# Modulation product of a two-layer diffusion step on four column tiles of TensorE

## What is computed

```python
def _adaln(cond, w, b):
    m = jax.nn.silu(cond) @ w + b
    return jnp.split(m[:, None, :], 3, axis=-1)

h = _rmsnorm(x, lp['norm_g']) * (1.0 + scale) + shift
z = h @ lp['w_in']
...
x = x + gate * (mixed @ lp['w_out'])
```

## Time and profile before

| what | value |
|---|---|
| median of the runs | 848.39 us |
| span of the profiled execution | 845.0 us (3.4 below the median) |
| TensorE busy | 712.7 us, 84% |
| VectorE busy | 605.8 us, 72% |
| ScalarE busy | 316.0 us, 37% |
| GpSimd busy | 172.6 us, 20% |
| moved by DMA | 117.64 MB, mean 139 GB/s |
| chain that ended last, by engine | TensorE 52%, VectorE 36%, ScalarE 3%, DMA 3% |

### The profile page before, as it was taken

How to read it: one execution, slowest core, us unless ns; L and a number is a source line. 1 busy time by engine, 2 the same in 40 slices (tenths; PEclk the granted TensorE clock), 3 DMA queues, 4 the chain that set the end, 5 groups by cost and what they waited for, 6 DMA issues and landing times.

```text
span 845.0 us, 9392 instructions
## 1 busy us (share of the span) xinstructions
PE 712.7 (84%) x3294; PEld 469.8 (56%) x3294; DVE 605.8 (72%) x1103; ACT 316.0 (37%) x563; POOL 172.6 (20%) x121
## 2 busy tenths in 40 slices
PE   4957899990779994988999999999907698999996
PEld 1145665550721533776778558655507456787785
DVE  3378689997355589768866554899973568888664
ACT  1244451111323322454655355401213433545552
POOL 1067449202000009033000100492020000000000
PEclk9979999995789997999999999999967698999999
DMA  6864335350067471554565475454220034555661
GB/s 208 282 146 118 125 128 173 110 145 28 3 155 232 141 239 61 150 150 146 154 184 168 147 236 165 137 166 118 73 99 1 26 99 124 176 174 155 195 177 55
DMA packets 79339, 117.64 MB, mean 139 GB/s; under 512 B 27437, under 2 KB 31869, under 8 KB 79293
## 3 DMA queue, kind: packets, MB, share of 16 engines
q1 hardware_dynamic: 78460, 116.52, 45.6%
q10 hardware_dynamic: 832, 0.53, 0.3%
HBM read 112.51 MB, written 1.38 MB: 135 GB/s over the span
## 4 chain that ended last, share of the span: by engine, by line
PE 52%; DVE 36%; ACT 3%; DMA 3%; issue 2%; SPq 2%; POOL 1%; DVEq 0%; ACTq 0%; POOLq 0%
PE proj L1032 11%; PE proj L1034 10%; PE proj L1033 10%; DVE H L1358 8%; PE proj L730 8%; DVE cvacc L1423 7%; DVE qkt L1358 7%; PE side L765 4%; PE proj L756 3%; DVE qM_split L1358 3%; PE side L963 2%; DVE wide_split L1358 2%; DMA raw<-in_w_ada 2%; DVE H L1575 2%; DVE gates_split L1358 2%
## 5 line engine op out<-in xcount | busy, mean ns | idle before, releaser
L756 PE MATMUL proj<-raw,hT 128*128 128x512 f32 (+1 forms) x320 | 125.1, 551 | 0.0
L1423 DVE SCALAR_TENSOR_TENSOR cvacc<-cvpad,taps,cvacc 128x256 f32<-128x256 f32 x240 | 123.1, 541 | 0.0
L1358 DVE TENSOR_TENSOR wide_split<-raw,wide_split 128x512 fp32r<-128x512 f32 x118 | 90.6, 773 | 41.4 <-ACT wide_split L1086 40.3
L1086 ACT ACTIVATE wide_split<-raw 128x512 fp32r<-128x512 f32 x118 | 74.4, 632 | 95.9 <-PE proj L1034 95.9
L756 PEld LDWEIGHTS proj<-raw,hT 128*128 128x128 f32 x320 | 60.3, 190 | 60.4 <-issue 58.4
L730 PE MATMUL proj<-raw,cond 128*2 128x512 f32 x192 | 88.8, 617 | 5.9 <-DMA raw<-in_w_ada 5.9
L1358 DVE TENSOR_TENSOR H<-H,qkt 128x128 f32<-128x128 f32 x128 | 75.5, 590 | 1.2
L1032 PE MATMUL proj<-wide_split,H_split 128*128 128x512 f32 x154 | 65.0, 422 | 13.2 <-DVE wide_split L1358 12.7
L1783 POOL TENSOR_SCALAR st<-st 128x1 f32<-128x1 f32 (+1 forms) x12 | 3.9, 324 | 336.9 <-DVE st L1692 148.7
L961 PE MATMUL side<-qM,Uz 128*64 128x64 f32 x128 | 20.5, 248 | 54.3 <-DVE HY L1676 54.3
L1033 PE MATMUL proj<-wide_split,H_split 128*128 128x512 f32 x154 | 62.8, 408 | 0.0
(11 more groups left out here) (235 smaller groups left out, 1491.1 us busy)
## 6 DMA issues: line engine op xcount, KB each, us to landing
raw<-in_w_in SPq DMA_DIRECT2D x104, 512.0 KB, 3.8
raw<-in_w_ada SPq DMA_DIRECT2D x48, 512.0 KB, 4.5
raw<-in_w_out SPq DMA_DIRECT2D x16, 512.0 KB, 4.2
raw<-in_w_ssm_glu SPq DMA_DIRECT2D x8, 512.0 KB, 5.2
raw<-in_w_ssm_out SPq DMA_DIRECT2D x8, 512.0 KB, 3.8
raw<-in_w_attn_out SPq DMA_DIRECT2D x8, 512.0 KB, 4.1
raw<-in_w_conv_out SPq DMA_DIRECT2D x8, 512.0 KB, 3.9
raw<-in_w_in SPq DMA_DIRECT2D x8, 256.0 KB, 2.8
```

Of the source, the lines that this page charges most:

```text
L756: m = T.matmul(proj.bank((l, u, s))[:, 0:n], lhs[:, s, kt, :], w[:, i, :], start=(kt == 0), stop=last)
L1086: S.activation(chunk_parts(m)[0], chunk_raw(m), ACT.Copy).then_inc(chunk_hi, 1)
L1358: return V.tensor_tensor(out, a, b, op)
L1423: m = V.scalar_tensor_tensor(acc, src, taps[:, t, j:j + 1], acc, ALU.mult, ALU.add)
```

## The change

The stationary operand `cond` is made 32 columns wide, the two conditioning vectors repeated 16 times. Each slab is multiplied in four matmuls of 256 columns; matmul j writes partitions 32j to 32j + 31 of one bank, which is column tile j of TensorE's array. ScalarE copies the bank in one piece of 128 x 256 into a buffer of its own, two full transposes bring it to columns, and VectorE's addition picks the two wanted rows out of each 32. The ScalarE waits on the shared buffer go. The order of stages is the same. The launch reserves a smaller scratch for DMA descriptors.

```diff
 ADA_PARTS = 3
-ADA_BANKS = D // W
+ADA_COLS = D // 4
+ADA_ROWS = P // 4
 MERGE_OF = {"A": 0, "B": 1, "C": 2}
...
         condrow = rows[:, 0, P:2 * P]
-        cond = sb("cond", [P, NS, DT])
+        cond = sb("cond", [P, DT, ADA_ROWS])
         h0 = sb("h0", [P, ROW])
...
 
-        adarow = th[:, 2:4, :].rearrange("p a b -> p (a b)")
+        adarow = sb("adarow", [P, ADA_COLS])
         qk = sb("qk", [P, NS, QK])
...
             if stg[0] == "ada":
-                proj_uses += [(stg + (b,), 1) for b in range(ADA_BANKS)]
+                proj_uses.append((stg, 1))
             proj_uses += [((l, u, s), 1) for u, _, _ in units_of(stg) for s in range(NS)]
...
             elif key[:-1] + (key[-1] + 1,) not in {q[0] for q in slabs}:
-                last = ADA_BANKS - 1 if key[0] == "ada" else NS - 1
-                slab_read.append((proj.full, proj.at[key[:-1] + (last,)][0] + 1))
+                bank_of = key[:-1] if key[0] == "ada" else key[:-1] + (NS - 1,)
+                slab_read.append((proj.full, proj.at[bank_of][0] + 1))
             else:
...
                 if kt == 0:
-                    for b in range(ADA_BANKS):
-                        proj.claim(pe, stg + (b,))
+                    proj.claim(pe, stg)
                 slab_landed(pe, stg + (kt,))
                 w = slab_view(stg + (kt,))
-                for b in range(ADA_BANKS):
-                    m = T.matmul(proj.bank(stg + (b,))[0:NS, :], cond[:, :, kt], w[:, 0, W * b:W * b + W],
-                                 start=(kt == 0), stop=(kt == DT - 1))
-                    if kt == DT - 1:
-                        m.then_inc(proj.full, 1)
-                if kt < DT - 1:
-                    m.then_inc(slab_used, 1)
+                for j in range(4):
+                    m = T.matmul(proj.bank(stg)[ADA_ROWS * j:ADA_ROWS * j + ADA_ROWS, 0:ADA_COLS], cond[:, kt, :],
+                                 w[:, 0, ADA_COLS * j:ADA_COLS * j + ADA_COLS], start=(kt == 0), stop=(kt == DT - 1))
+                m.then_inc(proj.full if kt == DT - 1 else slab_used, 1)
 
...
                 elif k == "adaT":
-                    for b in range(ADA_BANKS):
-                        proj.drained(pe, ("ada",) + stg[1:] + (b,))
+                    proj.drained(pe, ("ada",) + stg[1:])
                     side.claim(pe, stg)
-                    for t in range(DT):
-                        m = transpose(side.bank(stg)[:, NS * t:NS * t + NS], adarow[0:NS, P * t:P * t + P])
+                    for t in range(ADA_COLS // P):
+                        m = transpose(side.bank(stg)[:, P * t:P * t + P], adarow[:, P * t:P * t + P])
                     m.then_inc(side.full, 1)
...
                     side.filled(act, ("cond",))
-                    S.activation(cond[:, :, :].rearrange("p s t -> p (s t)"), side.bank(("cond",))[:, 64:80],
-                                 ACT.Silu).then_inc(cond_done, 1)
+                    S.activation(cond[:, :, :].rearrange("p t (i s) -> p s t i", s=NS),
+                                 side.bank(("cond",))[:, 64:80].rearrange("p (s t) -> p s t", s=NS).unsqueeze(3)
+                                 .to_broadcast([P, NS, DT, ADA_ROWS // NS]), ACT.Silu).then_inc(cond_done, 1)
                 elif k in ("ada", "adaEnd") and stg != OVER_EDGE:
...
                         side.filled(act, ("adaT",) + ada_parts[ada_parts.index(stg) - 1][1:])
-
-                    for u in {("ada", 0, 2): ("glua",), OVER_EDGE: ("wo0", "wo1")}.get(stg, ()):
-                        for s in range(NS):
-                            proj.drained(act, (0, u, s))
-                    for b in range(ADA_BANKS):
-                        key = stg + (b,)
-                        proj.filled(act, key)
-                        S.activation(adarow[0:NS, W * b:W * b + W], proj.bank(key)[0:NS, :],
-                                     ACT.Copy).then_inc(proj.freed(key), 1)
+                    proj.filled(act, stg)
+                    S.activation(adarow[:, :], proj.bank(stg)[:, 0:ADA_COLS], ACT.Copy).then_inc(proj.freed(stg), 1)
                 elif k == "cT":
...
                         high_parts(ahead(l, "cg"))
-                        if l:
-                            side.filled(act, ("adaT", l, 2))
-                    if stg[1] == "glub" and l + 1 < DEPTH:
-                        side.filled(act, ("adaT", l + 1, 1))
                     for s in range(NS):
...
                 elif k == "comb":
-                    if stg == ("comb", BRANCHES[0], 0) and l == 0:
-                        side.filled(act, ("adaT", 0, 2))
                     unit = stg[1] + str(stg[2])
...
                     part = slice(DT * c, DT * c + DT)
-                    tt_(ada[:, ll, part, :], side.bank(stg)[:, 0:NS * DT].rearrange("p (t s) -> p t s", s=NS),
-                        modc[:, ll, part].unsqueeze(2).to_broadcast([P, DT, NS]), ALU.add).then_inc(side.freed(stg), 1)
+                    tiles = ADA_COLS // P
+                    tt_(ada[:, ll, part, :].rearrange("p (j t) s -> p t j s", t=tiles),
+                        side.bank(stg)[:, 0:ADA_COLS].rearrange("p (t j q) -> p t j q", t=tiles, j=4)[:, :, :, 0:NS],
+                        modc[:, ll, part].rearrange("p (j t) -> p t j", t=tiles).unsqueeze(3)
+                        .to_broadcast([P, tiles, 4, NS]), ALU.add).then_inc(side.freed(stg), 1)
                     if c == 1:
...
 
-    nc = bacc.Bacc("TRN2", target_bir_lowering=False, num_devices=1)
+    nc = bacc.Bacc("TRN2", target_bir_lowering=False, num_devices=1, dynamic_dma_scratch_size=1024)
     arrays = {}
...
     def given(prefix, named):

```

## The result

The changed kernel takes **833.53 us** (median of 4 runs, 832.25 to 834.15); the kernel before took 847.51 beside it (4 runs, 846.03 to 848.56). The ratio is 0.9845, 95% interval 0.982 to 0.9869: faster by about 14 us. The forecast was 831.0, range 822 to 847. The profiled execution's span is 831.2 us against 845.0, so 13.8 us have to be found in the trace.

What follows compares the result with a forecast made beforehand. TensorE and DMA were taken as nearly balanced, the gain bounded by the DMA. Start 7, middle 7, after the GLU 0 and edge 3.3 sum to 17.3 us, carried to the 848.39 median: 831 us, range 822 to 847.

Steps and rivals of the forecast that it cites:

- The array: Modulation product: column tiles overlap in part, so a slab costs TensorE 0.86 us, between bounds of 0.43 and 2.59.
- Serial tiles: Modulation product: the four tiles run one after another, 1.71 us per slab as before; 846.3 us, chance 0.10.
- Exposed weight loads: Every product but four slabs: weight loads no longer hide, 2.59 us per slab instead of 1.71; 885.0 us, chance 0.07.
- Start: First 16 slabs and the input transposes behind them: the stretch shortens by 5.5 to 8.5 us, taken as 7.
- the limit that the prediction put at 5.5: Kernel start: SyncE issues its last w_ada slab, then b loads and first w_in slab, only some 5.5 us earlier.
- Middle: Middle of layer 0, 4 + 8 slabs: GELU transposes start at 269.0 instead of 275.6; 7 us with shorter transposes.
- after the GLU: Eight slabs behind the GLU: VectorE reaches its addition straight behind its taps without waiting; 0 us, 3 either way.
- side cases of the prediction: Middle of layer 0: GELU up to 2.6 us sooner; or slabs take 1.5 us and TensorE is late by a microsecond.
- 0.4 from fewer transposes: Middle of layer 0, at the GELU transposes: fewer transposes save 0.4 us, part of the 7 us there.
- Edge: Between the layers, 4 + 4 slabs: first half hides, first w_in slab released earlier, shorter transposes; 3.3 us.
- Release at 487.2, 3.1 earlier: Between the layers: the fifth slab's use releases the first w_in slab at 487.2 instead of 490.26; 3.1 us.
- The clock rival: TensorE, idle between slabs, drops to 1.2 GHz and a slab takes 1.71 us even overlapped; 843.5 us, chance 0.03.

Runs made afterwards that it cites:

- half slabs: Changed kernel loading only 512 of the 1024 columns of each w_ada slab, each half multiplied twice; 821.67 us, ratio 0.9711 to the kernel before.
- two-tile kernel: Changed kernel with each slab's four matmuls, from the second k-tile on, going in pairs to the first two column tiles; 832.39 us.
- one-tile: Changed kernel with all four matmuls of a slab, from the second k-tile on, going to the first column tile; 839.99 us.
- edge-filled kernel: Changed kernel with 10, 6 and 20 matmuls that nobody reads added in TensorE's idle time between the layers; 830.34 us.

## Why the prediction was right

**The array.** The forecast rested on tiles that overlap, at 0.86 us a slab between bounds of 0.43 and 2.59. It is 0.43 at the upper clock and at most 0.87 where 0.54 was granted (with half slabs, four in 3.47 us from 25.46), both under the transfer, so that the choice between them was without effect, as the two-tile kernel shows. That 0.87 is near the forecast's 0.86 is luck: the prediction had it from tiles that overlap in part. *Serial tiles* are refuted by the 288 us row (0.43, not 1.71). *Exposed weight loads* too: eight loads are hidden in each slab of that row. Here the Trainium skill ("TensorE: Matmul & The Clock Gate", Part 3, What overlaps and what doesn't) let loads pass a running matmul only where the row group differs; these share one row group and pass. The prediction's estimate from that part, 0.54 us a slab, was near in size but above what the row shows.

**Start, 7 us forecast, 5.7 measured** (4.1 to 5.7 over the profiles with the same start). First use of the fifth slab at 19.73 (landing 19.1 forecast), then 1.51 us a slab rather than 1.4, 11 x 0.11 = 1.2 us: the pace of four buffers; six have 1.28. The input transposes, forecast near 37 us, begin at 40.72, behind those of `pre`, 5.3 us sooner than before. What sets the term is the limit that the prediction put at 5.5, SyncE's advance and GpSimd behind it. SyncE, then GpSimd's first block:

```profile
40.77 16.14 SPq L663 DMA_DIRECT2D raw<-in_w_in  x6
...
66.16 2.71 POOL L1766 TENSOR_TENSOR pre<-tA,tB 128x1024 f32<-128x1024 f32 x1
```

The first w_in slab goes 4.4 us sooner than before and GpSimd's block ends 3.7 us sooner. The chain of waits now runs through the b loads and this block; before, it ran through the product and VectorE's splits.

**Middle, 7 us, and after the GLU, 0; together 6.2.** TensorE's and ScalarE's timelines:

```profile
262.21 1.08 PE L730 MATMUL proj<-raw,cond 128*32 128x256 f32 x8 [0.47 <-DMA raw<-in_w_ada]
263.23 1.97 PE L762 MATMUL side<-ident,mixed 128*128 128x128 f32 x8
264.99 0.63 PE L762 MATMUL side<-ident,adarow 128*128 128x128 f32 x2
265.42 1.14 PE L905 MATMUL side<-kz,qM 128*128 128x512 f32 x2
```

```profile
259.32 0.63 ACT L1296 ACTIVATE mixed<-mixed 128x512 f32<-128x512 f32 x1 [0.70 <-DVE mixed L1342]
```

With the start's 5.7 us added, so on the clock of the kernel before, the GELU transposes begin at 268.95; 269.0 was forecast. The number held, its reason did not: GELU is through at 259.95, 3 us ahead, and TensorE is last, because the twelve slabs took 1.52 us each. Both were side cases of the prediction (GELU sooner, slabs at 1.5), and that they met at the same number is luck. The "0.4 from fewer transposes" became 0.6 more: 2.2 us from 263.23 to 265.42, at a granted clock of 0.50, against 1.6. Behind the GLU, VectorE reaches its addition with no wait, right behind its taps, as in the earlier trace rows. The kernel was 11.8 us ahead when the GELU transposes ended (265.42, not 277.22) and is 11.7 ahead here, so nothing was gained or lost:

```profile
304.19 0.17 DVE L1342 TENSOR_TENSOR ada<-side,modc 128x16 f32<-128x16 f32 x1
```

**Edge, 3.3 us forecast, 0.1 measured: the step that failed.** "Release at 487.2, 3.1 earlier": the first w_in slab goes at 476.40, 13.9 us before, of which 11.9 had been gained already; 1.9 are the edge's own. Its transfer takes 3.8 us as before, but then the projection begins at half pace. TensorE's timeline and the chain of waits:

```profile
471.02 1.09 PE L762 MATMUL side<-ident,H 128*128 128x128 f32 x8 [2.45 <-DVE H L1516]
473.58 1.74 PE L762 MATMUL side<-ident,H 128*128 128x128 f32 x8 [1.46 <-DVE H L1516]
475.25 2.90 PE L730 MATMUL proj<-raw,cond 128*32 128x256 f32 x32
481.69 0.76 PE L1028 MATMUL proj<-qM_split,mixed_split 128*128 128x512 f32 x1 [3.53 <-DVE qM_split L1342]
```

```profile
476.40 3.77 DMA raw<-in_w_in
...
482.45 0.43 PE proj L1029
...
487.14 0.43 PE proj L1028
487.57 0.27 PE proj L1029
```

The second row's transposes take 1.74 us, where two overlapping fours of at most 0.60 had been costed, and twelve projection records take 0.43 us each instead of 0.23, 12 x 0.20 = 2.4 us. So the release was late by 1.2 us, and what it did gain was given back by the slow records. TensorE had been idle for 2.45, 1.46 and 3.53 us: the shorter product left it waiting just ahead of the work that needs its clock. Filling these waits gave 3.2 us back in the profile, and the one-tile and two-tile products, which keep it busy longer, are 2.1 and 1.8 us better at the edge.

**The clock rival** was half right: its event came (granted 0.50 in both large products), although at 64 us a half-busy TensorE had kept 1.00, so that window was no argument. Its price was wrong: it gave a slab 1.71 us "even overlapped", but four tiles at the lower clock need 0.87 to 1.08, and the DMA hid that. The clock cost where it was not looked for, at the edge.

**The sum.** 17.3 us were forecast, 13.8 measured in the profiles (14.0 between the medians): start and the rest of layer 0 short by 1.3 and 0.8, the edge by 3.2, and 1.8 came by the place of the low clock. Without that the kernel would have stood near 835, still in the range. So the forecast's place, 2.5 us from the median, is in part luck: 1.8 us that no term foresaw stand against the edge's missing 3.2.

## What to carry to other kernels

When an engine's part of a stage is halved, look up what the stage's next bound is and stop there: two tiles were as good as four, and a further 9 us lay in the number of buffers, which had been worth nothing while TensorE was the bound. A matmul stage made shorter can give its gain back in the next one, as at the edge here, where TensorE waited longer in between and started the next work at the lower clock. And a difference of 2 us far from the edit should be held against the granted clock of that stretch before it is credited to the edit.

## What the runs showed of the hardware that was not expected

Four column tiles of one row group run fp32 matmuls fully at once: 24 records of 256 columns and their loads in 1.50 us, 0.43 us for what takes 1.72 on one tile.

The granted clock does not tell the pace of short bursts between waits. In the start of the edge-filled kernel, where nothing was filled yet, the window reads 1.00, and yet each slab takes the 1.08 us that it takes at 0.50 in the changed kernel:

```profile
19.80:37.40 17.60, 12.01 (x92) 2.33 (x96) 8.62 (x33) 5.47 (x11) 1.47 (x4) 1.00 0.96 309
```

```profile
24.84 1.08 PE L730 MATMUL proj<-raw,cond 128*32 128x256 f32 x8 [0.17 <-DMA raw<-in_w_ada]
```

The last slab is done at 38.3 us there and at 37.4 here, so the product's end does not go with the granted clock either. The kernel before shows the same: granted 1.00 from 12 to 14 us, and steps of 0.83 us there.

115 matmuls that nobody reads, in one wait of 27 us per layer, shortened the kernel before by 0.7%.
